# A two-layer encoder trunk in fp32: attention and output projection of each layer put into one block, and the reciprocal standard deviations computed as exp(-0.5 log x) on ScalarE

## What is computed

```python
y = concat(heads) * silu(gate)              # both layers: 16 heads of 64 = 1024 features
y = einsum('bte,ed->btd', y, w_out)         # output projection, 1024 x 1024
x = x + rms_norm(y, g_post)
def rms_norm(x, g): return x * rsqrt(mean(x*x, axis=-1) + EPS) * g
```

## Time and profile before

| | us |
|---|---|
| three runs | 2401.09, 2399.99, 2398.0 (median 2399.99) |
| profiled execution | 2399.58 |
| its span on the core | 2397.7 |
| PE busy | 2121.7 (88%) |
| DVE, ACT, POOL busy | 1419.4, 1108.8, 1090.9 |
| mean granted TensorE clock | 0.939 |

### The profile page before, as it was taken

One profiled execution on the slowest core, in us unless ns is written; L12 is line 12 of the kernel. 1 busy time (PEld: TensorE's weight loads), 2 busy tenths in 40 slices (PEclk: granted clock), 3 DMA queues, 4 the chain that ended last, 5 costly groups with the idle time before them and its releaser, 6 DMA issues. The chain is left out here.

```text
span 2397.7 us, 25337 instructions
## 1 busy us (share of the span) xinstructions
PE 2121.7 (88%) x9396; PEld 1652.0 (69%) x9396; DVE 1419.4 (59%) x1938; ACT 1108.8 (46%) x1391; POOL 1090.9 (45%) x549
## 2 busy tenths in 40 slices
PE   6999988968999999994974699999699999996795
PEld 4777876846888877763863477788377777774584
DVE  7264146765777666644556487721477777773554
ACT  5132133322555666663314344333277777775331
POOL 5424344522555555552004477734266666664300
PEclk9999999986999999996997899999699999998898
DMA  4133488225554444317236033241423232312534
GB/s 158 36 121 123 132 268 224 83 89 127 116 116 113 113 116 112 86 27 249 81 112 231 36 114 115 97 123 66 101 62 73 66 73 66 73 41 82 190 106 132
DMA packets 196523, 266.60 MB, mean 111 GB/s; under 512 B 106592, under 2 KB 115424, under 8 KB 196400
## 3 DMA queue, kind: packets, MB, share of 16 engines
q1 hardware_dynamic: 196400, 264.97, 38.6%
HBM read 167.01 MB, written 97.91 MB: 110 GB/s over the span
## 5 line engine op out<-in xcount | busy, mean ns | idle before, releaser
L1738 POOL TENSOR_TENSOR c_PL<-c_PF,c_PH 128x1024 fp32r<-128x1024 f32 x128 | 307.2, 2400 | 198.0 <-ACT c_PH L1587 129.4
L1738 POOL TENSOR_TENSOR ab_PL<-ab_PF,ab_PH 128x1024 fp32r<-128x1024 f32 (+3 forms) x128 | 273.9, 2141 | 225.5 <-ACT ab_PH L1587 163.6
L1584 ACT ACTIVATE ab_PF<-ab_SA 128x1024 f32<-128x1024 f32 (+3 forms) x160 | 143.6, 898 | 215.2 <-PE ab_SA L1451 130.1
L938 PE MATMUL n_acc<-n_XH,n_wh 128*128 128x512 f32 x432 | 186.9, 433 | 61.8 <-DVE n_XL_r L1086 35.4
L1584 ACT ACTIVATE c_PF<-c_SA 128x1024 f32<-128x1024 f32 x160 | 164.0, 1025 | 141.3 <-PE c_SA L1486 139.6
L406 PE MATMUL e_acc<-e_XH,e_wh 128*128 128x512 f32 x480 | 197.4, 411 | 24.7 <-DVE e_XL_r L575 15.3
L1883 PE MATMUL o_acc<-o_XH,o_WH 128*128 128x512 f32 x384 | 153.4, 399 | 72.3 <-DVE Y_r L1926 72.3
L1634 DVE TENSOR_REDUCE c_MH<-c_SM 128x1 f32<-128x512 f32 x256 | 172.3, 686 | 75.9 <-PE c_SM L1416 75.8
L406 PE MATMUL e_acc<-e_XL_r,e_wh 128*128 128x512 f32 x480 | 192.6, 401 | 0.0
L406 PE MATMUL e_acc<-e_XH,e_wl 128*128 128x512 f32 x480 | 192.6, 401 | 0.0
L938 PE MATMUL n_acc<-n_XL_r,n_wh 128*128 128x512 f32 x432 | 173.8, 402 | 0.0
(11 more groups left out here) (248 smaller groups left out, 5555.3 us busy)
## 6 DMA issues: line engine op xcount, KB each, us to landing
o_G<-silu_gate SPq DMA_DIRECT2D x48, 256.0 KB, 2.8
c_Q<-qC_hi SPq DMA_DIRECT2D x32, 384.0 KB, 5.4
e_raw<-in_w_tiles SPq DMA_DIRECT2D x20, 512.0 KB, 3.8
n_raw<-in_w_tiles SPq DMA_DIRECT2D x18, 512.0 KB, 3.7
o_WL<-in_w_out SPq DMA_DIRECT2D x16, 512.0 KB, 6.2
e_XL<-in_xT SPq DMA_DIRECT2D x12, 512.0 KB, 10.3
silu_gate<-e_ta SPq DMA_DIRECT2D x24, 256.0 KB, 2.0
ab_Q<-qA_hi SPq DMA_DIRECT2D x16, 384.0 KB, 5.5
```

What stands on the lines that cost most here:

```text
L938: mm = nc.tensor.matmul(out, a[b][:, ks], x[:, k, cols(c)], start=(k + i == 0), stop=(k == KT - 1 and i == 2))
L1584: nc.scalar.activation(used(PF[p], h, s), used(SA, h, s), ACT.Exp).then_inc(e_done, 1)
L1738: nc.gpsimd.tensor_tensor(used(PL[p], h, s), used(PF[p], h, s), used(PH[p], h, s).bitcast(F32), ALU.subtract).then_inc(p_lo[0], 1)
```

## The change

- `output_projection` is gone. `attention` takes the layer number, gains, residual source and destination, and does the projection in its own block. The new tiles lie over buffers of attention that are no longer used (Q, K, V, P, OB, the bias tables) and over its PSUM banks: products go in turn to SM's and SA's two banks and OS, the sums to MT.
- The chunks come in the order (2, 0, 1), the sample first. The sample's eight tiles are gated, rounded and made low during heads 14 and 15: gate of tile n at the end of DVE's step `gate_slot`, its high part at the end of ACT's next step, its low part at the end of DVE's step after that. The weights 0 and 1 are rounded on ACT at steps 2 and 4 of head 15, their low parts made on POOL at its steps 4 and 8. SP loads six tiles, four gates and two weights in head 14, one more tile and weights 2 to 5 in head 15, the last tile after head 15's sample rows are stored. Tile 7 is gated after DVE's last step.
- PE makes product 0 before the last `pv`. The prompt chunks are loaded once head 15's prompt rows are stored.
- `deviation` is Ln and Exp on ACT and waits for `y_scaled`, no longer `y_ready`; DVE's reciprocal is gone. The same in `inner`, where the table load now stands first, the squares are summed after units 0, 2 and 4, and root(2) stands in ACT's loop at unit 2.
- `ar.recycle()` stands between `entry` and attention "ab", no longer behind that attention. `entry` itself is as before.

```diff
 # inner, PE, ACT and DVE
-                if n in (1, 3, 5):
+                if n in (0, 2, 4):
                     x_square_sum(n // 2)
...
-                nc.scalar.activation(out, sums[i % 2], ACT.Sqrt, bias=epst[:], scale=1.0 / count
-                                     ).then_inc(deviation, 1)
+                out = rstd[:, cols(i)]
+                nc.scalar.activation(out, sums[i % 2], ACT.Ln, bias=epst[:], scale=1.0 / D).then_inc(deviation, 1)
+                act.wait_ge(deviation, i + 1)
+                nc.scalar.activation(out, out, ACT.Exp, scale=-0.5).then_inc(rstd_ready, 1)
...
+            nc.scalar.preload_act_table_set("natural_log_exp_and_others")
             high_weights(0)
             split_x(0)
             high_weights(1)
             split_x(1)
-            root(0, rstd[:, cols(0)], D)
+            root(0)
             split_x(2)
-            root(1, rstd[:, cols(1)], D)
-            root(2, rstd[:, cols(2)], D)
-            nc.scalar.preload_act_table_set("natural_log_exp_and_others")
+            root(1)
             for n in range(N):
...
+                if n == 2:
+                    root(2)
...
-                nc.vector.reciprocal(x, x).then_inc(rstd_ready, 1)
 # attention
+    ORDER = (2, 0, 1)
+    NB, NG, EARLY = 5, 4, 6
+    LAST = NH - 1
+    gate_slot = {(LAST - 1, 3): 0, (LAST - 1, 5): 1, (LAST - 1, 7): 2, (LAST - 1, 9): 3,
+                 (LAST, 1): 4, (LAST, 3): 5, (LAST, 5): 6}
...
+        acc = [SM[:, 0:CH], SM[:, CH:2 * CH], SA[:, 0:CH], SA[:, CH:2 * CH], OS[:]]
+        sums = MT
 # SP, in the loop over h
+                if h == LAST - 1:
+                    stored_sample(12)
+                    load_x(0, 0, 0, 6)
+                    for n in range(NG):
+                        load_gate(n)
+                    load_w(0)
+                    load_w(1)
+                if h == LAST:
+                    for n in range(NG, KT):
+                        sp.wait_ge(x_gated, n - NG + 1)
+                        load_gate(n)
+                    stored_sample(14)
+                    load_x(1, 0, 6, 7)
+                    for t in range(2, EARLY):
+                        load_w(t)
+                if h == NH:
+                    for t in range(EARLY, KT):
+                        load_w(t)
...
+                if h == LAST:
+                    stored_sample(NH)
+                    load_x(2, 0, 7, 8)
+            for n in range(KT, KT + NG):
+                sp.wait_ge(x_gated, n - NG + 1)
+                load_gate(n)
             for b in range(2):
                 sp.wait_ge(st_prompt[b], 16 * (NH // 2))
...
+            load_x(3, 1, 0, 4)
+            load_x(4, 1, 4, KT)
+            load_res(0)
+            load_x(5, 2, 0, KT)
 # PE, after the loop over g
-            for g in range(G - LAG, G):
+            for g in range(G - LAG, G - 1):
                 pv(g)
+            product(0, 0)
+            pv(G - 1)
+            for t, g, a, p in stages():
+                if a is not None and (a, t) != (0, 0):
+                    product(a, t)
+                if t == 0 and p is not None:
+                    square_sum(p)
 # ACT
+            def deviation(j):
+                act.wait_ge(sum_ready, j + 1)
+                wait_count(act, y_scaled, j * KT)
+                nc.scalar.activation(rstd[:], sums[:], ACT.Ln, bias=epst[:], scale=1.0 / D).then_inc(y_log, 1)
+                act.wait_ge(y_log, j + 1)
+                nc.scalar.activation(rstd[:], rstd[:], ACT.Exp, scale=-0.5).then_inc(y_rstd, 1)
...
+                n = gated_before(h, s, 1)
+                if n is not None:
+                    high(n)
+                if (h, s) in ((LAST, 2), (LAST, 4)):
+                    high_weights(s // 2 - 1)
+            high(KT - 1)
+            high_weights(2)
+            high_weights(3)
             invert(NH - 1, 1)
+            for t, g, a, p in stages():
+                if a == 0 and t + 4 < KT:
+                    high_weights(t + 4)
+                if g is not None:
+                    high(g * KT + t)
...
 # DVE, at the end of step s of head h
+                n = gated_before(h, s, 2)
+                if n is not None:
+                    low_part(n)
+                if (h, s) in gate_slot:
+                    gate(gate_slot[h, s])
+            gate(KT - 1)
+            low_part(KT - 1)
             normalise(NH - 1, 1)
 # POOL
+                if (h, s) in ((LAST, 4), (LAST, 8)):
+                    low_weights(s // 4 - 1)
+            for t in range(2, KT):
+                low_weights(t)
 # build_trunk
         entry(nc, ar, S, A, ones, epst, gpre[0])
-        attention(nc, ar, "ab", A, S, ...)
-
         ar.recycle()
-            output_projection(nc, ar, 0, S, A, Y, gpost[0], ones, epst, A["xT"], S["X1"])
+        attention(nc, ar, 0, "ab", A, S, ..., gpost[0], ones, epst, A["xT"], S["X1"])
```

More of the change, by code:

```diff
@@ L1 @@
+import itertools
 from contextlib import ExitStack
@@ L1150, in _ @@
             split_x(1)
-            reciprocal(0, rstd[:, cols(0)])
             split_x(2)
             for n in range(N):
-                if n in (2, 4):
-                    reciprocal(n // 2, rstd[:, cols(n // 2)])
                 if n == v0:
@@ L1169, in _, with attention @@
                     nc.vector.tensor_copy(rtok[:], bank(v0 + 4)[:, 0:TT]).then_inc(tok_done, 1)
-def attention(nc, ar, tag, A, S, heads):
+def attention(nc, ar, l, tag, A, S, heads, gpost, ones, epst, xin, xout):
     NH, NS = len(heads), 10
@@ L1238, in attention @@
     st_sample = [ar.sem(f"{tag}_st_sample{i}") for i in range(2)]
+    w_in = [ar.sem(f"{tag}_w_in{t}") for t in range(KT)]
+    w_hi, w_lo = ar.sem(f"{tag}_w_hi"), ar.sem(f"{tag}_w_lo")
+    x_in = [ar.sem(f"{tag}_x_in_{n}") for n in ("sample", "sample6", "sample7", "0a", "0b", "1")]
+    g_in = [ar.sem(f"{tag}_g_in{i}") for i in range(NG)]
+    x_gated, x_hi, x_lo = (ar.sem(f"{tag}_x_{n}") for n in ("gated", "hi", "lo"))
+    acc_ready, y_raw, y_sq, y_added = (ar.sem(f"{tag}_{n}") for n in ("acc_ready", "y_raw", "y_sq", "y_added"))
+    sum_ready, y_log, y_rstd = (ar.sem(f"{tag}_{n}") for n in ("sum_ready", "y_log", "y_rstd"))
+    res_in = [ar.sem(f"{tag}_res_in{i}") for i in range(2)]
+    y_scaled, y_ready, y_out = (ar.sem(f"{tag}_{n}") for n in ("y_scaled", "y_ready", "y_out"))
     if NA:
@@ L1258, in attention @@
         negsel = sc.sb(f"{tag}_negsel", [AUG, AUG, P])
[L1259 to L1266 removed]
+        at_x = sc.here()
@@ new lines, in attention @@
+        XF, XL, XH, Y, WF, WL, WH = [], [], [], [], [], [], []
+        wide = (P, KT, CH)
+        for j, (low, high) in enumerate(((None, None), (at_p, at_p + 16384), (at_p + 32768, at_v))):
+            plain, rounded = (sc.both(f"{tag}_XL{j}", wide) if low is None else
+                              (sc.at(f"{tag}_XF{j}", wide, F32, low), sc.at(f"{tag}_XL{j}", wide, F32R, low)))
+            XF.append(plain)
+            XL.append(rounded)
+            XH.append(sc.sb(f"{tag}_XH{j}", wide, F32R) if high is None else sc.at(f"{tag}_XH{j}", wide, F32R, high))
@@ new lines, in attention @@
+        for j, place in enumerate((at_o, at_x, at_x + 16384)):
+            Y.append(sc.at(f"{tag}_Y{j}", wide, F32, place))
+        early = [at_q + o for o in (6144, 10240, 14336, 24576, 28672, 32768, 36864, 49152)]
+        late = [at_q + o for o in (0, 18432, 43008, 55296)]
+        for t in range(KT):
+            if t < 2:
+                plain, rounded = sc.both(f"{tag}_WL{t}", [P, D])
+                WH.append(sc.sb(f"{tag}_WH{t}", [P, D], F32R))
+            else:
+                low, high = early[2 * (t - 2):2 * (t - 1)] if t < EARLY else late[2 * (t - EARLY):2 * (t - EARLY + 1)]
+                plain, rounded = sc.at(f"{tag}_WF{t}", [P, D], F32, low), sc.at(f"{tag}_WL{t}", [P, D], F32R, low)
+                WH.append(sc.at(f"{tag}_WH{t}", [P, D], F32R, high))
+            WF.append(plain)
+            WL.append(rounded)
@@ L1296, in used, with cols, stages @@
             return t[:, 0:CH + v1 - v0]
+        def cols(c):
+            return slice(c * CH, (c + 1) * CH)
+        def stages():
+            for period in range(NC + 1):
+                g, a, p = (j if 0 <= j < NC else None for j in (period + 1, period, period - 1))
+                for t in range(KT + 2):
+                    live = t < KT
+                    yield (t, g if live else None, a if live else None, p)
         @block.sync
@@ L1559, in _, with product, square_sum @@
                     max_unit(h + 1, u)
-            for g in range(G - LAG, G):
-                pv(g)
+            def product(j, t):
+                n = j * KT + t
+                if t == 0:
+                    pe.wait_ge(x_lo, (j + 1) * KT)
+                if n == 0:
+                    pe.wait_ge(m_done, unit0[NH])
+                if n == 2:
+                    pe.wait_ge(e_done, G)
+                if n == 4:
+                    pe.wait_ge(o_sample, NH)
+                if j == 0:
+                    pe.wait_ge(w_lo, t + 1)
```

(18 more changed lines are left out.)

319 lines of the change are left out of this document (121 added, 198 removed).

## The result

2329.58 us (median of four executions, 2327.54 to 2331.81) against 2400.24 for the kernel before: a ratio of 0.9707, 95% interval 0.9690 to 0.9724, or 70.7 us less. The forecast was 2325 with a range of 2305 to 2350. The profiled execution took 2331.81, its span is 2329.9; it is the slowest of the four, so differences of single spans come out some 3 us too small.

A forecast was written before the change was run, and what follows sets the result against it. TensorE, busy 88% of the span, was taken as the bound, so time is won where it waits or runs slowly. Gains of 94.8 less costs of 20.4 gave 74.4 net, from 2399.6 to 2325 us; range 2305 to 2350.

The forecast's parts named there:

- The gap: Before each output projection: PE's 72.3 us of waiting go, and the slow-clock start, 4.2; gain 76.5.
- slower: Rival: short stops before products 0 and 8 keep TensorE at 1.2 GHz through the projections; up to 2523 us; chance 0.02.
- the edit does little: Rival: the first product still waits for the trip through DRAM, 30 us per layer; 2385 us; chance 0.01.
- Tile 7 and chunk 1: Around products 0 and 8: tile 7's late low part costs 3.6, chunk 1's later load 2.0, both layers.
- Product stage: Output projection's products: number of matmuls unchanged, PE does not stop inside; 70.9 less together with the gap.
- Tails: End of each projection: Ln and Exp replace Sqrt and reciprocal, scaling starts sooner; gain 3.4 per layer, 6.8.
- Inner: PE's wait for weight 2 in `inner` ends at 1340.5 instead of 1352.0; gain 11.5, bounds 4.6 and 15.
- The rival in which gates carry the stall: In `inner` the stall stays because gates, not roots, carry it: gain 4.6 instead of 11.5, 2332 us; chance 0.07.
- recycle: Moved from the covered gap to the start of attention "ab", on the path there; cost 1.0, bounds 0 and 2.
- ACT in the heads: Head 15: ACT's high parts of tiles and weights lengthen steps in layer 1; cost 2.8, bounds 0 and 6.
- DVE and POOL: Heads 14 and 15: new DVE instructions meet POOL subtractions and delay PE; cost 11.0, bounds 0 and 31.
- The rival in which each of the 14 instructions waits a whole one of POOL: Heads 14 and 15: port clashes cost 31 instead of 11, 2345 us; chance 0.18.

The follow-up runs named there:

- wait_per_tile: Changed kernel with PE waiting for each tile's low part just before using it, not for all eight at the product's start; 2319.70 us, timed again 2321.52.
- inner_before: Changed kernel with the sums of x, root and reciprocals of `inner` set back as they were before the change; 2341.70 us.
- dve_eight_columns: Changed kernel with DVE's gates and low parts of tiles 0 to 6 in heads 14 and 15 replaced by maxima over 8 columns; 2324.70 us.
- dve_one_input: Changed kernel with DVE's gates and low parts of tiles 0 to 6 replaced by equally long maxima reading one SBUF input; 2321.49 us.
- one_weight_per_gap: Changed kernel with per-tile low-part waits, gating at steps 5 and 9 over heads 12 to 15, POOL's weight splits at step 4 of heads 14, 15; 2310.37 us.
- act_eight_columns: Changed kernel with ACT's high parts of tiles 0 to 6 and of weights 0 and 1 cut to 8 columns; 2325.01 us.

## Why the prediction was right, and where its terms were off

- **The gap, 76.5.** The mechanism was right: PE's first product has its inputs, and 72.3 us of waiting are gone. The slow start is gone too; the windows of the products show a clock of 1.00. It was worth more than my 4.2: with its first dozen matmuls 0.43 us apart, product 0 took 2.3 us (layer 0) and 2.8 us (layer 1) longer than the next ones. So neither "slower" nor "the edit does little" came about.
- **Tile 7 and chunk 1, 3.6 and 2.0.** Measured as PE's waits: 2.6 + 2.8 = 5.4 and 1.1 + 0.6 = 1.7. The first was mis-sized: the low part of tile 7 came 0.8 to 1.0 us later than my sum of 1.8. In layer 1 POOL does the split of weight 1 right in front of the last PL, and it takes 3.40 us; so that PL ends 2.2 us behind the last `pv` but one, where I had 0.9, and the low part ends 0.55 behind the PL (2169.63 and 2169.08). I had not asked whether the wait has to stand in front of the whole product; `wait_per_tile` shows that nearly all of both is a matter of where it stands.
- **Product stage.** Together with the gap I had 70.9 less and there were 65.8. 1.5 is in the waits above, most of the rest in a step that I had taken as unchanged: the matmuls themselves came further apart at the same clock of 1.00 (last section), 1.3 us in period 0 and 0.5 in the later ones, in each layer.
- **Tails, 6.8.** 3.2 + 3.2 = 6.4; undone, 2.9 and 2.7 come back.
- **Inner, 11.5.** 12.6 measured, 12.1 by `inner_before`. The rival in which gates carry the stall is out. The 1.1 that my sum lacks lie at the start of the chain, in the end of DVE's sums of x, as timelines of DVE and ACT show:

```profile
1289.58 1.78 DVE L1093 TENSOR_TENSOR n_ssum<-n_ssum,n_sq 128x512 f32<-128x512 f32 x1
...
1291.99 0.63 ACT L1057 ACTIVATE n_tb<-n_ta 128x512 f32<-128x512 f32 x1 [1.83 <-DVE n_ta L1128]
```

  Counted from inner's first matmul and put on the time base of before, the sums end at 1321.0, where I had put 1322, and gate 0's Exp starts at 1321.6 instead of 1322.6. From there the chain takes what I had: the multiply of gate 4 stands at 1332.8 (1333.8 in my sum), and unit 6 follows 6.7 behind it. The Trainium skill ("ScalarE: Activation LUTs", what ACT_TABLE_LOAD costs) counts a drain besides the load; the gain would be 12.9 by that page, an estimate. That this is nearer to 12.6 is chance. The rows of before show the load of 1.28 us with Sqrt directly in front and Exp directly behind the earlier trace rows, and the 1.1 are found elsewhere.
- **recycle, 1.0.** 1.3, within what the start of attention varies by (26.7 to 28.2).
- **ACT in the heads, 2.8.** 2.5 in layer 1, by the two steps that remain in `dve_eight_columns`. For layer 0 I had let a longer step take it up; it cost 1.4 there (`dve_one_input`, head 15: 27.58 against 26.16, all of it in steps 2 and 4).
- **DVE and POOL, 11.0.** 7.6 to 8.2 in layer 1, where I had 7.0, and 1.5 in layer 0, where I had 4.0: 9.1 to 9.7. I had the sizes of head 14 and 15 the wrong way round in layer 1 (4.5 and 2.5; measured 3.1 and 4.5), since I took head 15 as roomy: DVE is, but POOL with the two weights is not. The rival in which each of the 14 instructions waits a whole one of POOL is out: the 16 gates and low parts took 27.2 us instead of the 10.9 of sixteen undisturbed ones, 1.0 extra on average. The heads lost 7.6, and some 2 of these are a cost that my term did not have at all: the lower clock behind PE's waits. In layer 0, where no such stretch lies in the two heads, the same work cost 1.5.

The costs in the heads thus sum to 13.6 against my 13.8, with the shares of the layers off in both directions; that the sum came out so close is luck. With the product stage 5.1 short, inner 1.1 better, the tails 0.4 and recycle 0.3 worse, the terms sum to 69.9 instead of 74.4; the medians say 70.7.

The Trainium skill ("SBUF — State Buffer", engine ports) describes an exclusive lock in which the loser blocks for the whole instruction. The traces agree for DVE: a gate that meets a subtraction ends 0.56 behind it, and the new instructions show no wait when they read one input from SBUF. Three in a row took 2.80, 2.88 and 2.83, one of POOL's each. They agree for POOL too, when DVE is the first. Timelines of DVE and POOL in head 15 of the changed kernel:

```profile
2162.57 1.48 DVE L1883 TENSOR_TENSOR c_PL<-c_PF,c_PH 128x1024 fp32r<-128x1024 f32 x1 [1.87 <-ACT c_PH L1780]
...
2162.92 3.40 POOL L1997 TENSOR_TENSOR c_WL_r<-c_WL,c_WH 128x1024 fp32r<-128x1024 f32 x1
```

POOL's split of a weight, 2.35 alone, takes 3.40: it ends 2.27 behind DVE's end at 2164.05. Subtractions of POOL that start while a low part of DVE runs take 2.68 to 2.89 in that head, instead of 2.40.

## What to carry to other kernels

When work is slipped into the loop of another stage, look up for each slot what the *other* user of the same port does there, not how idle the engine is: fourteen instructions of 0.68 us cost 8 us in layer 1 at the ends of steps and under 2 in the gaps of GpSimd, and one instruction of GpSimd left in such a gap cost 6.6 in one head. Look at the granted clock behind each wait as well: a wait of TensorE of 2 us in head 14 cost 1.6 more afterwards. Put a wait at the operand that needs it and not at the head of the product that reads eight. And measure a loop's stretch by the spacing of one instruction per step; it gave 0.1 us where spans gave 3.

## What the runs showed that I had not expected

Matmuls of the same form came at different intervals at a granted clock of 1.00. First and last of the rows of one pattern (every third matmul), PE's timeline, layer 0's products, first in the changed kernel (21 rows, 60 intervals), then in the one before (22 rows, 63 intervals):

```profile
1095.27 0.40 PE L1717 MATMUL ab_SA<-ab_XH,ab_WH 128*128 128x512 f32 x1
...
1109.33 0.40 PE L1717 MATMUL ab_OS<-ab_XH,ab_WH 128*128 128x512 f32 x1
```

```profile
1130.24 0.39 PE L1883 MATMUL o_acc<-o_XH,o_WH 128*128 128x512 f32 x1
...
1144.52 0.39 PE L1883 MATMUL o_acc<-o_XH,o_WH 128*128 128x512 f32 x1
```

14.06 / 60 = 0.234 us and 14.28 / 63 = 0.227. A product of 24 takes 5.62 us instead of 5.44 from product 2 to 7, and the first two of each later period 0.15 more than before; the others are at 0.227 again. These values are the same to 0.01 us in both layers and in the traces of `wait_per_tile_timed` and `one_weight_per_gap`, so it isn't chance. What causes it (other addresses, the engines beside it) was not tried.

The first head of layer 0 took between 29.96 and 34.43 us in kernels that don't differ there, while every later head repeats to 0.1. It goes with the clock, which is at its 1.2 GHz level when the head begins. In the head of 29.96 us (`act_eight_columns`) the granted clock stays at 0.50 for the first 3.8 us, in those of 33.78 to 34.43 for 14.1 to 15.5; in layer 1 it is 0.4 us in the shortest first head (27.04) and 3.4 to 3.6 in the longest (28.12). About the same part of the head, windows of the changed kernel and of `act_eight_columns`:

```profile
572.00:580.90 8.90, 8.72 (x30) 7.02 (x31) 4.06 (x12) 3.22 (x5) 4.79 (x3) 0.50 0.06 19
...
572.10:581.50 9.40, 8.47 (x57) 7.17 (x56) 4.87 (x20) 5.27 (x7) 5.30 (x3) 1.00 0.12 36
```

Why the clock came back earlier in one execution was not looked into. It is one reason why single executions of one kernel differ by some us.
